# Hybrid attention layer on one core: first two tiles in column halves, small inputs on ScalarE's queue, one cast on GpSimd

## The reference

```
h = concatenate([meta, x], axis=1)
h = layer_norm(h, ln_emb_g, ln_emb_b)      # mean, variance over 1024 columns; * g + b
proj = h @ w_in                            # 1024 x 3560; the first two blocks of 128 columns used are cq
bias = rel_bias[t5_bucket(t_pos - sel)]    # 32 buckets x 8 heads
```

## Time and profile before

| | us |
|---|---|
| median of 3 runs (329.17 to 330.17) | 329.18 |
| profiled execution | 329.63 |
| its span, first to last instruction | 327.8 |
| TensorE busy | 317.7 (97%) |
| VectorE, ScalarE, GpSimd busy | 236.9, 172.8, 196.6 |
| mean granted clock of TensorE | 0.995 |

### The profile page before, as it was taken

One profiled execution on the slowest core, in us unless ns is written; L12 is line 12 of the kernel. 1 busy time (PEld: TensorE's weight loads), 2 busy tenths in 40 slices (PEclk: granted clock), 3 DMA queues, 4 the chain that ended last, 5 costly groups with the idle time before them and its releaser, 6 DMA issues.

```text
span 327.8 us, 6250 instructions
## 1 busy us (share of the span) xinstructions
PE 317.7 (97%) x2134; PEld 276.7 (84%) x2134; DVE 236.9 (72%) x630; ACT 172.8 (53%) x389; POOL 196.6 (60%) x243
## 2 busy tenths in 40 slices
PE   8999999999999999999999999999999999999991
PEld 7799987888778888987988987897978898998991
DVE  5984810279955799989995995578787866564786
ACT  4876843362442455367454753777587752732230
POOL 6552999989322262439430898689869582570222
PEclk9999999999999999999999999999999999999998
DMA  7564333239422122202300052333323110140033
GB/s 250 220 200 179 130 128 119 81 138 287 134 98 85 58 78 74 80 3 80 131 10 8 22 177 95 94 101 81 98 86 97 65 34 34 65 130 0 2 128 128
DMA packets 11997, 32.86 MB, mean 100 GB/s; under 512 B 2440, under 2 KB 2824, under 8 KB 11968
## 3 DMA queue, kind: packets, MB, share of 16 engines
q1 hardware_dynamic: 9232, 26.89, 24.2%
q10 hardware_dynamic: 2736, 5.59, 5.8%
HBM read 29.83 MB, written 4.81 MB: 106 GB/s over the span
## 4 chain that ended last, share of the span: by engine, by line
PE 90%; DVE 5%; ACT 1%; DMA 1%; issue 1%; ACTq 0%; DVEq 0%; SPq 0%
PE ps_j L1486 54%; PE ps_t L1486 8%; PE ps_o L1723 6%; PE ps_s L1674 6%; PE ps_s L1678 4%; PE ps_s L1647 3%; PE ps_t L1693 2%; PE ps_j L1540 2%; PE ps_t L1698 2%; PE ps_j L1563 1%; PE ps_j L1441 1%; DMA res<-in_x 1%; PE ps_j L1431 1%; DVE st L1037 1%; PE ps_j L1424 1%
## 5 line engine op out<-in xcount | busy, mean ns | idle before, releaser
L588 POOL TENSOR_TENSOR wl<-raw,wh 128x1024 fp32r<-128x1024 f32 (+2 forms) x33 | 78.1, 2375 | 47.2 <-ACT wh L595 47.0
L1486 PE MATMUL ps_j<-hh,wh 128*128 128x512 f32 (+2 forms) x208 | 72.9, 351 | 0.2 <-DVE qs L1158 0.2
L1486 PE MATMUL ps_j<-hl,wh 128*128 128x512 f32 (+2 forms) x208 | 72.5, 348 | 0.0
L1486 PE MATMUL ps_j<-hh,wl 128*128 128x512 f32 (+2 forms) x208 | 72.1, 347 | 0.0
L748 POOL TENSOR_SCALAR pr<-pr,rden 128x528 f32<-128x528 f32 (+1 forms) x64 | 35.2, 570 | 49.0 <-DVE rden L1299 49.0
L1486 PEld LDWEIGHTS ps_j<-hh,wh 128*128 128x128 f32 (+1 forms) x208 | 38.7, 186 | 6.2 <-issue 0.3
L989 ACT ACTIVATE pr<-pr,mn 128x528 f32<-128x528 f32 (+1 forms) x64 | 36.0, 565 | 14.2 <-DVE mn L1288 14.1
L1486 PEld LDWEIGHTS ps_j<-hh,wl 128*128 128x128 f32 (+1 forms) x208 | 38.8, 187 | 5.1
L1486 PEld LDWEIGHTS ps_j<-hl,wh 128*128 128x128 f32 (+1 forms) x208 | 38.8, 186 | 5.0
L595 ACT ACTIVATE wh<-raw 128x1024 fp32r<-128x1024 f32 (+2 forms) x34 | 34.9, 1040 | 0.5 <-DMA raw<-in_weights 0.5
L766 POOL TENSOR_TENSOR bm<-bias,mask 128x144 f32<-128x144 f32 (+3 forms) x32 | 27.5, 892 | 0.0
(11 more groups left out here) (287 smaller groups left out, 845.4 us busy)
## 6 DMA issues: line engine op xcount, KB each, us to landing
raw<-in_weights SPq DMA_DIRECT2D x35, 512.0 KB, 3.3
bias_by_distance<-bias_vector ACTq DMA_DIRECT2D x1, 2624.0 KB, 13.8
bias<-bias_by_distance ACTq DMA_DIRECT2D x8, 264.0 KB, 3.0
res<-in_x SPq DMA_DIRECT2D x4, 512.0 KB, 4.6
out<-res SPq DMA_DIRECT2D x3, 512.0 KB, 2.6
raw<-in_weights SPq DMA_DIRECT2D x5, 256.0 KB, 6.4
pt<-in_ln_emb_g SPq DMA_DIRECT2D x1, 512.0 KB, 5.1
pt<-in_ln_emb_b SPq DMA_DIRECT2D x1, 512.0 KB, 6.0
```

The source lines that it names most:

```text
L588: eng.tensor_tensor(ring_of(False, b), raw_of(b), ring_of(True, b).bitcast(F32), ALU.subtract).then_inc(done, 1)
L1486: last = pe.matmul(dst, a, b, start=n == 0 and part[0], stop=n == count - 1 and part[1])
```

## The change

SyncE loads tiles 0 and 1 as four transfers of 128 x 512, left and right halves on semaphores of their own (`x_in`, `x_right`), then the weights' first halves, and only then tiles 2 and 3. Meta tokens, gains, `rb` and the one-hot table are issued by ScalarE, ahead of its table load. VectorE no longer makes `nmr`: ScalarE does it for the meta tokens and tiles 0, 2 and 3 (`negative`, `scaled_mean`), and scales each tile in two column halves (`normal(n, half, done)`). The cast of block 0's first half goes from ScalarE to GpSimd, behind VectorE's scaling of tile 1. On TensorE the vector of biases comes behind 17 fillers, then 3 fillers, the meta tokens' transposes and 4 fillers.

```diff
@@ SyncE
-            sp.dma_start(x_meta, meta).then_inc(x_in[4], 16)
-            tile_in(0)
-            tile_in(1)
-            sp.dma_start(gain[:, :], gains).then_inc(par_in, 16)
-            sp.dma_start(rb[:, :], rel_bias).then_inc(par_in, 16)
-            sp.dma_start(oh_sb, onehot).then_inc(oh_in, 16)
-            tile_in(2)
+            for t in range(2):
+                sp.dma_start(res[:, t, 0:512], x[0, t * P:(t + 1) * P, 0:512]).then_inc(x_in[t], 16)
+                sp.dma_start(res[:, t, 512:1024], x[0, t * P:(t + 1) * P, 512:1024]).then_inc(x_right[t], 16)
...
                 if half == 0:
+                    tile_in(2)
                     tile_in(3)
@@ GpSimd
-            pool.wait_ge(w_first_act, 1)
+            pool.wait_ge(xn_dve, 2)
+            pool.wait_ge(first_in[0], 16)
+            pool.tensor_copy(wh[:, 0:4, 0:P], raw[:, 0, 0:4, :]).then_inc(w_high_pool, 1)
+            pool.wait_ge(w_high_pool, 1)
             pool.wait_ge(w_high_dve, 1)
             first_low(0)
@@ ScalarE
+            def scaled_mean(n, done):
+                t, r = TILES[n]
+                act.wait_ge(shift, n + 1)
+                act.wait_ge(center, done - 1)
+                act.activation(nmr[0:r, t:t + 1], nmr[0:r, t:t + 1], ACT.Copy, scale=rstd[0:r, t:t + 1]).then_inc(center, 1)
+            def normal(n, half, done):
+                t, r = TILES[n]
+                src = (x_meta if t == 4 else res[:, t, :])[:, 512 * half:512 * half + 512]
+                act.wait_ge(center, done)
                 act.activation(src, src, ACT.Identity, bias=nmr[0:r, t:t + 1],
                                scale=rstd[0:r, t:t + 1]).then_inc(xn_act, 1)
...
+            act.dma_start(x_meta, meta).then_inc(x_in[4], 16)
+            act.dma_start(gain[:, :], gains).then_inc(par_in, 16)
+            act.dma_start(rb[:, :], rel_bias).then_inc(par_in, 16)
+            act.dma_start(oh_sb, onehot).then_inc(oh_in, 16)
             deviation(0)
-            normal(0, 2)
+            negative(0)
+            scaled_mean(0, 2)
+            normal(0, 0, 2)
             deviation(1)
-            normal(1, 4)
+            negative(1)
+            normal(0, 1, 2)
+            scaled_mean(1, 4)
             deviation(2)
-            act.wait_ge(first_in[0], 16)
-            act.activation(wh[:, 0:4, 0:P], raw[:, 0, 0:4, :], ACT.Copy).then_inc(w_first_act, 1)
+            normal(1, 0, 4)
+            normal(1, 1, 4)
             act.wait_ge(par_in, 32)
             gains_of(0)
             high(0)
+            high(1)
+            gains_of(2)
             deviation(3)
             negative(3)
-            high(1)
-            gains_of(2)
             high(2)
-            normal(3, 6)
+            scaled_mean(3, 6)
+            normal(3, 0, 6)
+            normal(3, 1, 6)
+            high(3)
             deviation(4)
             negative(4)
-            high(3)
-            normal(4, 7)
+            scaled_mean(4, 8)
+            normal(4, 0, 8)
+            normal(4, 1, 8)
@@ VectorE: the statistic of a right half waits for its own load, and inverse(n) makes no nmr
+                elif t < 2:
+                    dve.wait_ge(x_right[t], 16)
@@ TensorE
             pe.wait_ge(made, 2)
-            busy(30)
-            pe.wait_ge(xn_act, 1)
+            busy(17)
+            pe.wait_ge(oh_in, 16)
+            pe.wait_ge(par_in, 32)
+            for n, (a, b) in enumerate([(0, 512), (512, VECW)]):
+                pe.matmul(vec_bank(n), rb[:, :], oh_sb[:, a:b], start=True, stop=True).then_inc(vec_mm, 1)
+            busy(3)
+            pe.wait_ge(xn_act, 2)
...
+            busy(4)
```

More of the change, by code:

```diff
@@ L433, in build @@
         x_in = [sem(f"x_in{t}") for t in range(5)]
+        x_right = [sem(f"x_right{t}") for t in range(2)]
         par_in = sem("par_in")
@@ L450, in build @@
         w_high_pool = sem("w_high_pool")
-        w_first_act = sem("w_first_act")
         xn_dve = sem("xn_dve")
@@ L579, in high_made @@
             if b == FIRST_BLOCKS:
-                eng.wait_ge(w_high_pool, 3)
+                eng.wait_ge(w_high_pool, 4)
             else:
@@ L702, in _ @@
                 pool.tensor_copy(wh[:, 4:8, b * P:b * P + P], raw[:, b, 4:8, :]).then_inc(w_high_pool, 1)
-            pool.wait_ge(w_high_pool, 2)
+            pool.wait_ge(w_high_pool, 3)
             first_low(2)
@@ L792, in negative @@
             def negative(n):
-                t = TILES[n][0]
-                act.activation(nmr[:, t:t + 1], mv[:, t, 0:1], ACT.Copy, scale=-1.0).then_inc(center, 1)
-            def normal(n, need):
                 t, r = TILES[n]
[L800 to L805, removed]
+                act.activation(nmr[0:r, t:t + 1], mv[0:r, t, 0:1], ACT.Copy, scale=-1.0).then_inc(center, 1)
+            def scaled_mean(n, done):
[7 more added lines that the diff above has]
+                act.wait_ge(center, done)
                 act.activation(src, src, ACT.Identity, bias=nmr[0:r, t:t + 1],
@@ L1018, in _ @@
                         act.wait_ge(centred, 2 * t + 2)
-                        act.wait_ge(shift, 7 + t + 1)
+                        act.wait_ge(shift, 5 + t + 1)
                         y = res[:, t, :]
@@ L1040, in stat, with inverse @@
                     dve.bn_aggr(mv[0:r, t, :], st[0:r, t, :, :].rearrange("p a b -> p (a b)")).then_inc(stats, 1)
-            def inverse(n, done):
+            def inverse(n):
                 t, r = TILES[n]
@@ L1046, in inverse @@
                 dve.reciprocal(rstd[0:r, t:t + 1], rstd[0:r, t:t + 1]).then_inc(shift, 1)
[L1047 to L1051, removed]
+                if n == 2:
+                    dve.wait_ge(shift, 3)
                     for x in (0, 512):
@@ L1075, in _ @@
             stat(1, 0)
-            inverse(0, 1)
+            inverse(0)
             stat(1, 1)
             stat(2, 0)
-            inverse(1, 3)
+            inverse(1)
             stat(2, 1)
-            stat(3, 0)
-            inverse(2, 5)
-            stat(3, 1)
+            inverse(2)
             dve.wait_ge(first_in[1], 16)
@@ L1087, in _ @@
             gains_of(1)
-            stat(4, 0)
-            inverse(3, 6)
-            stat(4, 1)
+            stat(3, 0)
+            stat(3, 1)
             low(0)
             gains_of(3)
+            inverse(3)
             low(1)
-            inverse(4, 7)
+            stat(4, 0)
+            stat(4, 1)
             low(2)
+            inverse(4)
             low(3)
@@ L1395, in _ @@
             last.then_inc(x_t, 1)
-            pe.wait_ge(oh_in, 16)
-            pe.wait_ge(par_in, 32)
-            for n, (a, b) in enumerate([(0, 512), (512, VECW)]):
-                pe.matmul(vec_bank(n), rb[:, :], oh_sb[:, a:b], start=True, stop=True).then_inc(vec_mm, 1)
+            busy(4)
             def spread(u):
@@ L1415, in high @@
                 a = 256 * (u // 4)
-                if u % 4 < 2:
-                    pe.wait_ge(w_first_act, 1)
-                    pe.wait_ge(w_high_dve, 1)
-                else:
-                    pe.wait_ge(w_high_pool, 2)
+                pe.wait_ge(w_high_dve, 1)
+                pe.wait_ge(w_high_pool, 1 if u % 4 < 2 else 3)
                 pe.wait_ge(h_high, u + 1)
@@ L1444, in low @@
                         last.then_inc(job_mm, 1)
-            busy(6)
-            pe.wait_ge(xn_act, 2)
+            pe.wait_ge(xn_act, 3)
             pe.wait_ge(xn_dve, 1)
@@ L1450, in _ @@
             spread(1)
+            pe.wait_ge(xn_act, 4)
             pe.wait_ge(xn_dve, 2)
@@ L1458, in _ @@
             high(3)
-            pe.wait_ge(xn_act, 4)
+            low(2)
+            pe.wait_ge(xn_act, 7)
             spread(4)
             spread(5)
-            low(2)
+            low(3)
+            pe.wait_ge(xn_act, 8)
             spread(6)
-            low(3)
             spread(7)
```

2 lines of the change are left out of this document (1 added, 1 removed).

## The result

| | before | after |
|---|---|---|
| median (5 runs each, in turns on one chip) | 329.54 (329.17 to 330.17) | 332.65 (332.56 to 333.14) |
| profiled execution | 329.63 | 332.65 |
| its span | 327.8 | 330.7 |

The ratio is 1.0095, its 95% interval 1.0084 to 1.0107: 3.1 us slower, where 1.2 us faster was forecast.

What follows compares the result with a forecast made beforehand. TensorE was taken as the bound, busy 317.7 of 327.8 us and without long waits after about 27 us. The head's 1.35 us less 0.15 lost gave 1.2 us off the median 329.18: 328.0, range 327.3 to 329.4.

Steps and rivals of the forecast that it cites:

- I take 5.2, halfway: One-hot table on ScalarE's queue: expected to land at 5.2 us, between 4.2 and 6.1, releasing TensorE's bias product.
- rival D: TensorE's head: idle from 5.2 until the table, spacing stays 0.21 us; 1 to 2 us slower, chance 0.10.
- less what the rest catches up: Deduction from first transposes 1.7 us late and slow spacing in the spreads, leaving +1 to +2 us.
- Part 1: Head up to the first transposes: they start at 8.8 us instead of 10.17, 1.35 us earlier.
- The wait for tile 0: VectorE's head: half a tile lands near 3.6 us, so the 0.25 us wait goes.
- the statistic at 8.24: VectorE's head: this statistic goes behind the scaling, bringing the scaling 0.6 us earlier.
- Part 2: ScalarE's 0.63 us weight cast goes to GpSimd: no cost on the path, up to 0.6 us if weights come late.
- The lock: Port pair shared by VectorE and GpSimd: their casts come together, so one waits 0.37 us for the other.
- Part 3: First transposes to 27.05 us: tile 3's chain starts spread(4) at 17.65 instead of 18.51; 1.2 us gained in sum.
- 0.1 for H4: Deduction for TensorE's high product of unit 3: its hh comes out just as TensorE reaches it, 0.1 us.
- B: Earlier start eaten before 18.51 us by late meta tokens or VectorE's statistics; 0.3 to 0.9 us stay, chance 0.28.
- C: First transposes wait for fillers again, table at 6.1 us or later; gain 0 to 0.3 us, chance 0.12.

Runs made afterwards that it cites:

- the table first: Changed kernel with meta tokens leading SyncE's queue and ScalarE's queue issuing one-hot table, rel_bias, then gains; 17 fillers: 330.54 us, ratio 1.0046.
- the order: Changed kernel with 25 fillers and the work for tiles 2 and 3 reordered on VectorE, ScalarE and TensorE: 329.33 us, ratio 0.9998.
- the product behind the transposes: The order kernel with meta tokens on SyncE, 30 and 6 fillers, bias product moved behind the first four groups of transposes: 329.19 us, ratio 0.9993.
- the last experiment: The product behind the transposes, without GpSimd's wait for VectorE's scaling of tile 1 ahead of its cast: 329.21 us, ratio 0.9989.
- 21 fillers: Changed kernel with 21 fillers instead of 17 ahead of the bias product: 330.96 us, ratio 1.0044.
- everything with few fillers: Loads of the table first and orders of the order kernel, 18 fillers, 2 behind the product, none behind the meta transposes: 330.34 us, ratio 1.0017.
- meta tokens back on SyncE: The order kernel with only the meta tokens' load moved back in front of SyncE's queue: 329.18 us, ratio 0.9990.
- the product's old place: Changed kernel with 30 fillers and the bias product put back behind the meta tokens' transposes, then 2 fillers: 330.27 us, ratio 1.0037.

## Why the prediction was wrong

**The step that failed** is "I take 5.2, halfway" for the table's landing, and with it 17 fillers "out by 5.2" followed at once by the product. It landed at 6.56. I had bounded it at 4.2 to 6.1, each end from a landing in the earlier trace rows, the upper one taken from the 4.0 us in SyncE's queue; on ScalarE's queue it took 4.4, and 6.0 in the old kernel with that queue. The gap of 1.2 us that followed is rival D's mechanism, at the landing ("about 6.6") from which I let it decide. I gave it 0.10, since only 75 KB stood ahead of the table in its own queue. But while it was on its way the DMA engines were full with the tiles of the other queue: 310 GB/s at a share of 1.02 from 2 to 5 us, 319 at 1.03 from 5.4 to 6.6. The Trainium skill (DMA: Bandwidth & Descriptors, "Issuing engines are not separate DMA queues") had said that the DMAs of both queues run on the same engines and interleave, and the runs agree, with 2.9 and 3.3 us for the meta tokens where they took 2.1, and 4.4 for the table where it took 4.0. I had let that rule move the landing only to 6.1.

**The landing was not the whole of it.** The sum also had the clock up at about 7 us, as in the kernel before, whatever TensorE did until then, and kept from there on. In "the table first" the wait before the product was 0.38 us, the clock was up even earlier, and it was taken back: first transposes at 9.24 and at half pace, 330.54 and not 328.0 (with the wait for `hh` still in it). What TensorE's idle time does to its clock stood in D alone.

**D's price was too small as well**: 330.2 to 331.2 forecast, 332.65 measured. Its first transposes at 11.9 were close (11.58). Not priced were the further groups at half pace (1.17 us), for which I wrote only "for part of the spreads", and the wait for `hh`; and "less what the rest catches up" was mostly not there.

**Part 1, the other terms.** The wait for tile 0 went, as said; but the 0.8 us of later meta tokens, which only rival B had, took more than that. VectorE scaled at 8.81, not 7.97. Most of that, 0.7 us, is the later start of tile 0's statistics (5.17, where the sum had about 4.45). Moving away the statistic at 8.24, entered at 0.6, gave 0.3: a wait of 0.36 us for ScalarE's root stands in its place. Table load 2.61 to 3.89, as said and free. Two ScalarE halves take 1.50 us, the whole tile took 1.24: a half costs 0.80 to 0.81, not 0.62 to 0.65, since half the columns don't halve it. The Trainium skill (ScalarE: Activation LUTs, "What ACT_TABLE_LOAD costs") says so: a fixed 186 ns, 93 more for each operand that is one number per partition, and 0.833 ns per column. With two such operands that would be 0.80 and 1.23 us, an estimate from the page, and the rows agree with both. ScalarE's tile 0 was ready at 9.99, not 8.8, covered only because TensorE was later still.

**Part 2** held in its result, no cost on the path, but partly by luck: TensorE came late to it. In the kernels with the head repaired it waits 0.60 us for GpSimd's `wl` at 15.80 (the order), and the chain of "the product behind the transposes" goes through GpSimd for 5.8 us. The lock was mis-sized. The two casts met (9.73 and 9.88), GpSimd's took 0.74, which is 0.13 more than its 0.61 alone, not 0.37 more (spans on GpSimd are rough); it began only 0.27 before VectorE's end. VectorE's took 0.42 here and 0.42 in the last experiment, where the two did not meet.

**Part 3** had "0.1 for H4" where 0.65 stood. I followed tile 3's chain and took `hh` of unit 3 to come out just as TensorE reaches it, though it now stands behind both halves of a scaling on ScalarE (17.93 to 19.36). With TensorE back at full pace that wait is most of what remained, and the order experiment took it away. spread(4) began at 21.57, not 17.65.

**B** was true of the queue: 0.8 us by itself in the kernel before. In the order kernel, bringing the meta tokens back moved the ratio by 0.0008, inside the intervals. **C** was not seen: it had the table at 6.1 and a gap without a price. And the gain itself: where a repaired kernel reached it in a trace (8.84 and 25.86, forecast 8.8 and about 25.8) the medians show 0.3 to 0.5 us of it, not 1.2. Behind the head only 0.1 us goes (from the next block's start in the chain to the end of the span it is 300.8 us, before 300.75), but the profiled execution was the fastest of its kind. What the rest is wasn't settled. One slip changes nothing: the chances of "faster", 0.42 and 0.10, make 0.52 and not 0.53.

## What to carry to other kernels

Work that nobody reads, at the start of a kernel, is not spare time: fill until past the latest landing of what TensorE wants next; here, real work 0.5 us later without the gap ended 2.6 us earlier. A number of fillers is not a time: 25 of them took 5.60 us in one profile and 4.68 in another, as the clock rose later or earlier. Moving small loads to a second queue did not take them past the large ones; price their landing by all bytes in flight, and issue first what is needed first. When a step is cut in halves, price the half from a row of that size, and see what on the same engine stands behind the second one.

## What the hardware showed that I had not expected

- TensorE's clock is taken back after it was granted: 0.50 or 0.51 in windows of 3 to 6 us, with TensorE busy all of the 6, behind idle times of 0.3 to 1.3 us in three kernels (21 fillers, the table first, everything with few fillers). Yet gaps of 0.72 and 0.28 us (meta tokens back on SyncE), 0.68 (the order), 0.71 (the product behind the transposes), 1.02 and 0.37 (GpSimd's cast set free) and 1.17 (the product's old place) went without it in the profiled executions. So the length of a gap does not decide; what does was not settled. In the changed kernel, and in the kernel before with 17 fillers, the gap came ahead of the first rise, and the rise then came only near 14 and near 13 us.
- The moment of the first rise differs from profile to profile with the same fillers before it, from about 4.5 to about 7.5 us. Four kernels with a gap (17 fillers in the kernel before, 21 fillers, the table first, the product's old place) scatter by 1.8 to 2.3 us, those with 24 or more fillers ahead of an early product by 0.5 to 1.3; but three other kernels with gaps in their profiles (everything with few fillers, and the two with the product behind the transposes) scatter by only 0.7 to 1.4, so a gap does not always bring the scatter. The changed kernel itself paid in each of its 5 runs, within 0.6 us. The Trainium skill (TensorE: Matmul & The Clock Gate, "What's actually happening") says that this moment differs from run to run of one kernel, and profiles of kernels alike up to there agree; it also says that the ramp costs under 1% of a typical span and that one should not fit to a count. Its being late was 0.8% here (2.6 of 330 us), within that bound, and it turned the change's sign.
- A ScalarE scaling of 512 columns takes 0.80 us with 128 partitions and 0.81 with 16; one of 1024 columns takes 1.24.
